# One decoder step on one core: order of loads and waits in the output stage, and expert biases split on 128 partitions

## What is computed

```python
h = modulate(x, g_mix, shift1, scale1)           # RMSNorm * (1 + scale) + shift
y = mixer(h) @ w_out                             # GLA heads and NSA heads, one output projection
x = x + gate1 * y                                # first residual
h2 = modulate(x, g_ffn, shift2, scale2)          # rmsnorm(x, g_ffn) * (1 + scale2) + shift2
f = moe_ffn(h2, ...)                             # top 4 of 32 experts, each with three biases
x = x + gate2 * f                                # second residual ("ffn gate")

def moe_ffn(h, ...):                             # per token and chosen expert e
    logits = h @ w_router + b_router
    gate = min(x_b @ w_gate[e] + b_gate[e], 7)
    up = clip(x_b @ w_up[e] + b_up[e], -7, 7)
    return ((up + 1) * gate * sigmoid(1.702 * gate)) @ w_down[e] + b_down[e]
```

## Time and profile before

| what | value |
|---|---|
| device time, median of 3 runs | 1878.17 us (1877.72 to 1880.02) |
| span of the profiled execution | 1877.7 us (no device time of its own is listed; the lowest run is 1877.72) |
| busy: PE, DVE, ACT, POOL | 91%, 77%, 58%, 15% of the span |
| output stage | about 545 to 671 us |
| expert stage | about 671 to 1854 us |
| bytes moved | 516.55 MB, mean 275 GB/s |

### The profile page before, as it was taken

One profiled execution on the slowest core, in us unless ns is written; L12 is line 12 of the kernel. 1 busy time (PEld: TensorE's weight loads), 2 busy tenths in 40 slices (PEclk: granted clock), 3 DMA queues, 4 the chain that ended last, 5 costly groups with the idle time before them and its releaser, 6 DMA issues. The chain is left out here.

```text
span 1877.7 us, 27275 instructions
## 1 busy us (share of the span) xinstructions
PE 1706.9 (91%) x9073; PEld 1329.3 (71%) x9073; DVE 1438.2 (77%) x1320; ACT 1094.9 (58%) x1034; POOL 278.0 (15%) x312
## 2 busy tenths in 40 slices
PE   4999878888778869999999999999999999999982
PEld 3777666555554457888888888888888888888861
DVE  4422374576435678999999999999999999999983
ACT  3211343354322345777777777777777777777762
POOL 0000102300104000212212212211111121221110
PEclk9999879799898769999999999999999999999996
DMA  9354374500145267999999999999999999999963
GB/s 351 137 193 156 87 219 128 191 13 1 51 165 161 100 246 292 368 373 372 362 374 375 361 371 374 369 371 371 367 370 375 366 362 387 369 364 379 363 249 119
DMA packets 112071, 516.55 MB, mean 275 GB/s; under 512 B 25853, under 2 KB 47117, under 8 KB 59242
## 3 DMA queue, kind: packets, MB, share of 16 engines
q1 hardware_dynamic: 99098, 485.77, 69.0%
q0 software_dynamic: 12912, 29.98, 5.9%
HBM read 502.69 MB, written 31.81 MB: 285 GB/s over the span
## 5 line engine op out<-in xcount | busy, mean ns | idle before, releaser
L2609 PE MATMUL banks<-split 128*128 128x512 f32 x4608 | 1082.1, 394 | 1.0 <-DVE split L2768 1.0
L2609 PEld LDWEIGHTS banks<-split 128*128 128x128 f32 x4608 | 863.9, 189 | 194.5 <-issue 14.9
L2768 DVE TENSOR_TENSOR split<-expert_buffers,split 128x2048 fp32r<-128x2048 f32 x384 | 867.2, 2285 | 58.1 <-ACT split L2699 56.1
L2699 ACT ACTIVATE split<-expert_buffers 128x2048 fp32r<-128x2048 f32 x384 | 733.4, 1918 | 246.2 <-PE banks L2609 232.3
L2549 POOL TENSOR_TENSOR expert_buffers<-routing 128x1 f32<-128x1 f32 x63 | 59.7, 948 | 917.8 <-PE banks L2616 531.0
L496 PE MATMUL banks<-w_in_high,hT_high 128*128 128x476 f32 x192 | 75.9, 395 | 4.4 <-DVE hT_low L397 4.4
L2772 DVE TENSOR_TENSOR split<-banks,split 128x1024 fp32r<-128x1024 f32 x64 | 77.7, 1214 | 2.0 <-ACT split L2702 2.0
L424 DVE COPY arena<-banks 128x476 f32<-128x476 f32 x12 | 7.8, 654 | 91.1 <-PE banks L496 91.0
L496 PE MATMUL banks<-w_in_high,hT_low 128*128 128x476 f32 x192 | 73.4, 382 | 0.0
L2702 ACT ACTIVATE split<-banks 128x1024 fp32r<-128x1024 f32 x64 | 64.6, 1010 | 8.8 <-PE banks L2616 8.8
L2144 PE MATMUL banks<-arena 128*128 128x512 f32 (+1 forms) x160 | 68.2, 641 | 1.3 <-DMA arena<-in_w_out 1.3
(11 more groups left out here) (364 smaller groups left out, 1698.4 us busy)
## 6 DMA issues: line engine op xcount, KB each, us to landing
expert_buffers<-in_w_gate SPq DMA_DIRECT2D x128, 1024.0 KB, 7.4
expert_buffers<-in_w_up SPq DMA_DIRECT2D x128, 1024.0 KB, 5.1
expert_buffers<-in_w_down SPq DMA_DIRECT2D x128, 1024.0 KB, 8.4
arena<-in_w_ada SPq DMA_DIRECT2D x16, 1024.0 KB, 4.8
w_in_landing<-in_w_in SPq DMA_DIRECT2D x6, 1904.0 KB, 15.7
arena<-in_w_ada SPq DMA_DIRECT2D x4, 2048.0 KB, 17.1
arena<-in_x_prompt SPq DMA_DIRECT2D x8, 512.0 KB, 10.2
arena<-in_cache_cmp POOLq DMA_DIRECT2D x32, 128.0 KB, 3.3
```

Of the source, the lines that this page charges most:

```text
L2609: last = pe.matmul(ps[:, bank + c, :], x[:, kt * P:(kt + 1) * P].bitcast(F32R), wt.bitcast(F32R), start=False, stop=(kt == KT - 1 and x is ...
L2699: act.activation(high[:, j % RING_Q].bitcast(F32R), v, ACT.Copy).then_inc(s_high, 1)
L2768: dve.tensor_tensor(rest[:, j % RING_Q].bitcast(F32R), v, high[:, j % RING_Q], ALU.subtract).then_inc(s_rest, 1)
```

## The change

1. SP's loads stand in another order: gate1 alone, x of tile 0, g_ffn, shift and scale of the prompt, x of tiles 1 to 4, b_router, eight sample loads of three rows. The nine loads of gate2 now stand behind the biases, with a semaphore of their own (`s_gate2`) that SP waits for at the end of the stage.
2. VectorE no longer waits for all of x, g_ffn and all modulation rows ahead of its first tile. Each tile waits for its own x (`s_x[t]`) ahead of the addition, the first for gate1 (`s_exp[0]`), and `scales` for the prompt stands behind the first residual, with the waits for shift, scale and g_ffn.
3. The biases are loaded as 128 partitions (expert and quarter) of 3 x 256 in place of 32 partitions of 3 x 1024. POOL's five instructions have 768 elements in place of 3072, on 128 partitions. `bias_parts` has the layout [expert, quarter, part, matrix, 256], so each load of the expert stage takes two pieces of 256 for each of the 3 rows.

```diff
@@ -2016,21 +2016,23 @@
...
     upper = Stack(core, core.z1 + NT * D, ARENA)
-    b32 = placed.take(3 * D)
+    BQ = D * NE // P
+    b32 = placed.take(3 * BQ)
     zero = upper.take(D)
-    bparts = upper.take(3 * 3 * D // 2).bitcast(BF16).rearrange("p (a n) -> p a n", a=3)
+    bparts = upper.take(3 * 3 * BQ // 2).bitcast(BF16).rearrange("p (a n) -> p a n", a=3)
...
-    core.bias_d = nc.dram_tensor("bias_parts", [NE, 3, 3 * D], BF16).ap()
-
...
+    core.bias_d = nc.dram_tensor("bias_parts", [NE, D // BQ, 3, 3, BQ], BF16).ap()
+
...
-    s_x, s_first = core.sem("x_again_in"), core.sem("first_rows_ready")
+    s_x, s_first = [core.sem(f"x_again_in{t}") for t in range(NT)], core.sem("first_rows_ready")
+    s_exp, s_gate2 = [core.sem(f"prompt_mod_in{i}") for i in range(2)], core.sem("ffn_gates_in")
...
@@ -2047,25 +2049,31 @@
...
             sp.dma_start(mix[0:NSEQ * TS, ST, 512:1024].rearrange("p (q d) -> p q d", d=HD),
                          core.nsa_d.rearrange("h g b t d -> (b t) (h g) d")).then_inc(s_back, 16)
-            for t, (t0, n) in enumerate(TILES):
+            def load_x(t):
+                t0, n = TILES[t]
                 src = io["x_prompt"][0, t0:t0 + n, :] if t < ST else io["x_sample"].rearrange("b t d -> (b t) d")
-                sp.dma_start(x[0:n, t, :], src).then_inc(s_x, 16)
+                sp.dma_start(x[0:n, t, :], src).then_inc(s_x[t], 16)
+
+            sp.dma_start(ex[:, 0, 0, :], core.mod_d[0:1, 2 * D:3 * D].to_broadcast([P, D])).then_inc(s_exp[0], 16)
+            load_x(0)
+            sp.dma_start(gffn, io["g_ffn"].to_broadcast([P, D])).then_inc(s_w, 16)
+            sp.dma_start(ex[:, 0, 1:3, :].rearrange("p v n -> p (v n)"), core.mod_d[0:1, 3 * D:5 * D].to_broadcast([P, 2 * D])
+                         ).then_inc(s_exp[1], 16)
+            for t in range(1, NT):
+                load_x(t)
             sp.dma_start(br, io["b_router"].to_broadcast([P, NE])).then_inc(s_rt, 16)
-
-            sp.dma_start(ex[:, 0, :, :].rearrange("p v n -> p (v n)"), core.mod_d[0:1, 2 * D:5 * D].to_broadcast([P, 3 * D])
-                         ).then_inc(s_exp, 16)
-            sp.dma_start(gate2[:, 0, :], core.mod_d[0:1, 5 * D:6 * D].to_broadcast([P, D])).then_inc(s_exp, 16)
-            sp.dma_start(gffn, io["g_ffn"].to_broadcast([P, D])).then_inc(s_w, 16)
             for s in range(NSEQ):
                 rows = slice(TS * s, TS * s + TS)
                 sp.dma_start(ex[rows, 1, :, :].rearrange("p v n -> p (v n)"),
                              core.mod_d[1 + s:2 + s, 2 * D:5 * D].to_broadcast([TS, 3 * D])).then_inc(s_exps, 16)
-                sp.dma_start(gate2[rows, 1, :], core.mod_d[1 + s:2 + s, 5 * D:6 * D].to_broadcast([TS, D])
-                             ).then_inc(s_exps, 16)
             sp.wait_ge(s_mta, NT)
             sp.wait_ge(s_mtd, NT)
             for i, name in enumerate(("b_gate", "b_up", "b_down")):
-                sp.dma_start(b32[0:NE, i * D:(i + 1) * D], io[name][0]).then_inc(s_b, 16)
+                sp.dma_start(b32[:, i * BQ:(i + 1) * BQ], io[name][0].rearrange("e (q n) -> (e q) n", n=BQ)).then_inc(s_b, 16)
+            sp.dma_start(gate2[:, 0, :], core.mod_d[0:1, 5 * D:6 * D].to_broadcast([P, D])).then_inc(s_gate2, 16)
+            for s in range(NSEQ):
+                sp.dma_start(gate2[TS * s:TS * s + TS, 1, :], core.mod_d[1 + s:2 + s, 5 * D:6 * D].to_broadcast([TS, D])
+                             ).then_inc(s_gate2, 16)
...
             sp.wait_ge(s_zero, 1)
             for t0, n in TILES:
@@ -2080,6 +2088,7 @@
             for u in range(2):
                 sp.wait_ge(s_h2o[u], 16 * ((NT + 1 - u) // 2))
             sp.wait_ge(s_zo, 16 * NT)
+            sp.wait_ge(s_gate2, 16 * (1 + NSEQ))
...
@@ -2089,15 +2098,15 @@
...
             pool.wait_ge(s_b, 48)
-            b = b32[0:NE, :]
             for a in range(3):
                 if a < 2:
-                    link(pool.tensor_copy(bparts[0:NE, a, :], b))
-                    link(pool.tensor_tensor(b, b, bparts[0:NE, a, :], ALU.subtract))
+                    link(pool.tensor_copy(bparts[:, a, :], b32))
+                    link(pool.tensor_tensor(b32, b32, bparts[:, a, :], ALU.subtract))
                 else:
-                    pool.tensor_copy(bparts[0:NE, a, :], b).then_inc(s_bp, 1)
+                    pool.tensor_copy(bparts[:, a, :], b32).then_inc(s_bp, 1)
             pool.wait_ge(s_bp, 1)
-            pool.dma_start(core.bias_d, bparts[0:NE, :, :]).then_inc(s_bo, 16)
+            pool.dma_start(core.bias_d.rearrange("e q a m n -> (e q) (a m n)"), bparts.rearrange("p a n -> p (a n)")
+                           ).then_inc(s_bo, 16)
...
@@ -2267,17 +2276,15 @@
...
             def scales(who, rows):
...
-                dve.wait_ge(s_exps if who else s_exp, 32 * NSEQ if who else 32)
+                dve.wait_ge(s_exps if who else s_exp[1], 16 * NSEQ if who else 16)
+                if not who:
+                    dve.wait_ge(s_w, 16)
                 dve.scalar_tensor_tensor(ex[0:rows, who, 2, :], ex[0:rows, who, 2, :], 1.0, gffn[0:rows, :], ALU.add, ALU.mult
                                          ).then_inc(s_exd, 1)
             for t, (t0, n) in enumerate(TILES):
                 dve.wait_ge(s_mt, t + 1)
                 dve.tensor_copy(mixT[:, 4:8, t0:t0 + n],
                                 ps[:, 2 * (t % 2) + 1, 0:4 * n].rearrange("p (k n) -> p k n", k=4)).then_inc(s_mtd, 1)
-            dve.wait_ge(s_w, 16)
-            dve.wait_ge(s_x, 16 * NT)
-            scales(0, P)
-
...
@@ -2329,7 +2336,8 @@
                 who = int(t == ST)
                 if who:
                     scales(1, n)
-                dve.wait_ge(s_exd, 1 + who)
+                if not who:
+                    dve.wait_ge(s_exp[0], 16)
                 hh = h2[0:n, t % 2, :]
                 dve.wait_ge(s_yp, t + 1)
                 if t >= 2:
@@ -2342,7 +2350,11 @@
                 else:
                     link(dve.tensor_tensor(hh, ps[0:n, 4 + 2 * (t % 2):6 + 2 * (t % 2), :].rearrange("p b n -> p (b n)"),
                                            ex[0:n, who, 0, :], ALU.mult))
+                dve.wait_ge(s_x[t], 16)
                 dve.tensor_tensor(x[0:n, t, :], x[0:n, t, :], hh, ALU.add).then_inc(s_res, 1)
+                if t == 0:
+                    scales(0, P)
+                dve.wait_ge(s_exd, 1 + who)
                 if t >= 1:
                     choose(t - 1)
                 dve.wait_ge(s_rs, t + 1)
@@ -2494,9 +2506,9 @@
                     sp.wait_ge(s_used, used)
                 for c in range(2):
                     r0 = bias_row(m, c)
-                    sp.dma_start(bias[r0:r0 + 3, m // 2, :],
-                                 core.bias_d[bass.ds(e, 1), :, m * D + c * 512:m * D + (c + 1) * 512]
-                                 .rearrange("e a n -> (e a) n")).then_inc(s_bias[m], 16)
+                    sp.dma_start(bias[r0:r0 + 3, m // 2, :].rearrange("a (q n) -> a q n", q=2),
+                                 core.bias_d[bass.ds(e, 1), 2 * c:2 * c + 2, :, m, :].rearrange("e q a n -> (e a) q n")
+                                 ).then_inc(s_bias[m], 16)
...
```

4 lines of the change are left out of this document (2 added, 2 removed).

## The result

| | median us | runs | lowest to highest |
|---|---|---|---|
| before (the three runs above and four more) | 1879.10 | 7 | 1877.72 to 1882.98 |
| change | 1870.77 | 7 | 1867.81 to 1876.89 |
| ratio, 95% interval | 0.9946 | | 0.9926 to 0.9967 |

The change is faster by 0.54% (0.33% to 0.74%): 8.3 us by the two medians, about 10 by the ratio. The prediction had the direction and the mechanism, and a gain of 5.6 us. What came is a gain of 8 to 10 us where 5.6 was priced. The profiled run took 1870.29 us, with a span of 1868.6 and a span of 1877.7 before: 9.1 us less.

What follows compares the result with a forecast made beforehand. PE bounds the expert loop, which starts when the output stage and barrier allow. Gains of 3.39 (idle) and 2.44 (transposes, router), with -0.26 (projection), sum to 5.57 us: from 1878.17 to 1872.6 us, range 1869.2 to 1876.0.

Steps and rivals of the forecast that it cites:

- What bounds it, and the path: PE sets the expert loop's pace; the output stage's end sets its start, and the late g_ffn load delays that stage.
- Tile 0: In the output stage, h2 of the first tile is ready at 575.9 us in place of 584.39; PE wants it at 581.14.
- The loads: Output stage: new load order priced at 0; at the bad end h2 is ready at 578.8, 2.4 us ahead of PE.
- POOL: Biases' split in the output stage takes 5.7 us instead of 22.8; unchanged, it would take the whole gain back.
- The rival of an unshortened split: POOL takes 22.8 us on 128 partitions too, PE waits at tile 1: gain about 0, 1877.7 to 1878.2 us; chance 0.06.
- -0.26 us at projection 2: Projection behind tile 0's transposes and router takes 15.66 us where it took 15.40, its first half 8.81 where 8.40.
- rival 1: PE's clock stays up in tile 2's projection: first half 7.11 us, 1.70 less than 8.81; total 1870.9 us; chance 0.13.
- the range's two dips to either side: Two clock dips of 1.7 us more or fewer on PE, giving 1869.2 to 1876.0 us.
- 3.39 us of idle time: PE's wait between projection 1 and tile 0's transposes goes: they begin at 581.14 instead of 584.53.
- The expert loop: Bias loads in six pieces of 512 bytes, not three of 1024, cost 0, with 21.7 us in hand.
- rival 4: Bias rows land late in the expert loop, each microsecond costing PE one per expert: 1904.6 us at 22.7; chance 0.04.
- Rival 2: More dips, a late stage part not moving along, or POOL meeting VectorE costs 2 to 4 us: about 1875.5; chance 0.12.

Runs made afterwards that it cites:

- the fill of the handovers: Changed kernel with one overwritten matmul between PE's transposes and router at each handover but the last: 1869.64 us, ratio 0.9937.

## Why the prediction was right in kind and short in size

**What bounds it, and the path: right.** The expert loop is as full as before, the time behind the stage has changed by 0.6 us, and most of what the stage lost is what PE no longer waited, and its low clock behind that wait. The kernel without the moved waits gained nothing.

**Tile 0: right.** 575.9 was worked out, 576.6 measured, with the scale beside ScalarE at no cost.

**The loads: right in price, wrong in bound.** The order is worth 1.7 us by the medians (1872.42 against 1870.77) and 1.3 by the ratios, whose intervals overlap, so it isn't told from 0. The sentence "each is in by the time the old order had g_ffn in, 574.98" failed: landings move between executions, and with the old order the scale waited until 578.62, beyond a reserve of 2.4 us. A landing read from one execution is a sample, not a bound.

**POOL: right.** 5.7 us and 1.6 to 1.7 each were worked out; 6.8 and 1.64 were measured. That an unchanged split would take the gain back held for 5.4 to 7 us of it. A quarter of the length on four times the partitions took a quarter of the time in the additions, as the fills had suggested. The rival of an unshortened split fell. For its cost, the cast of 0.82 us took 1.70 beside VectorE, and VectorE's shift 6.9 beside an addition; the Trainium skill ("SBUF — State Buffer", the section on two separate sides) describes a port pair of the two engines that one holds for a whole instruction. By that rule the length of POOL's instruction is what counts, and the traces agree: 6.91 beside 6.86, and at most 2.40 in any run with the short split.

**The first term that failed: -0.26 us at projection 2.** I took the handover of tile 1, with a dip behind it, as the pattern for that of tile 0. In the change the first half took 7.11 us, not 8.81. The period from the transposes of tile 0 to those of tile 1 was 17.97 us (599.75 - 581.78), not 19.78, and for that case the prediction named the clock as the place to look. It is the case of rival 1, which had a chance of 0.13. The half at projection 3 came clean too, which no rival had; only the range's two dips to either side allowed for it. Both together take 5.57 to 9.0 us, 1869.2: the very end of the range. The rival's mechanism, no idle gap and so no dip, is only half borne out. Behind a wait of PE of 1.8 us or more ahead of tile 0's transposes the half took 8.40 to 9.04 us in all seven profiles without a fill of the handover (7.11 with one). With a wait of 0.7 us or none it took 7.11 in six profiles and 8.81 in two, the runs with one and with three matmuls ahead. But at the second handover, with the same kind of gap, eleven of fourteen profiles without a fill show 8.81. The dip there comes and goes from run to run: the change lacks it in its first profile and has it in the second. So of the 3.4 us, 1.7 at projection 2 belong to the change in most executions, and the 1.7 at projection 3 in the first profile are luck.

**The second, and the one that a range of dips could not cover: 3.39 us of idle time.** It was read correctly and was one sample of a range from 3.1 to 8.3 us. The mean of the three idle times (3.06, 3.40, 8.33) is 4.9 us; with that and a clean half behind it (1.47 in place of -0.26) the sum is 8.8 us, near the 9.3 of the mean stages. That is worked out afterwards from few executions, and how much each of the two terms gives on average is not shown more closely. From the trace of the kernel before alone the spread could have been suspected: a load of 512 KB took 18.6 us from its issue at 556.36 to landing, with a full queue ahead and behind. I gave that landing no range, and so the forecast had none on its most important term.

**The expert loop: right**, no wait; rival 4 fell. Rival 2, half the gain lost, fell as well.

**Left open.** Why g_ffn's landing varies by 5 us between executions of one kernel; why the start of projection 0 varies by 7; what decides whether a handover dips; and whether the fill of the handovers, with the lowest median (1869.64), is faster than the change, which its interval doesn't tell.

## What to carry to other kernels

A wait for everything, ahead of a loop's first use of anything, costs what the last load costs. Put each wait at the instruction that reads the data, before reordering loads: here the waits gave the gain and the order of loads a reserve. When a wait is removed, ask which long instruction it was hiding, and shorten that in the same change: the short split alone gave nothing, and the moved waits with the new order but the long split kept only 0.2% of the 0.5%. Take the size of a wait on a transfer from several executions, and give it a range if there is only one.

## What was unexpected of the hardware

- The landing of one load, at the same place in the same kernel, 22.8 and 27.7 us behind the start of the same matmuls. With sixteen small loads that are issued after it held back it was 21.6, with five stores held too 20.3; one profile each, so that these move it is likely but not shown.
- Handovers with the same work, the same busy share of PE and the full granted clock are followed by 1.00 in one place and 0.80 in another. The second handover of the kernel before, and the half behind it:

```profile
606.50:610.60 4.10, 2.93 (x24) 2.74 (x25) 4.03 (x4) 1.02 (x1) 3.06 (x2) 1.00 0.62 195
610.60:619.30 8.70, 8.70 (x20) 3.69 (x20) 6.78 (x24) 4.70 (x9) 0.00 (x0) 0.80 0.32 98
```

  PE was busy for 2.93 of 4.1 us ahead of this 0.80. The change has the same 2.93 of 4.1 us at 1.00 at this handover in both of its profiles (599.70 to 603.80, and 600.20 to 604.30), and the half behind it has 1.00 in the first and 0.80 in the second. What tells the two apart no run here shows. The Trainium skill ("TensorE: Matmul & The Clock Gate", Part 1) ties the low clock to an idle engine; with one matmul more in each gap, 3.69 of 4.0 us busy, no half behind one dipped, which agrees with it, though in the six handovers of two profiles only.
- One matmul between transposes and router was enough to have the router at the full clock (1.87 us) even behind an idle time of 8.50 us (with four more ahead of the idle time), where it took 3.62 behind 1.82 to 8.33 without it.
